# Linear attention of a decoder layer: the products of two heads in one group, alternating between two PSUM banks, in new slots

## The chip, the cores and the metric

One core of a Trainium2 chip runs the whole layer. The metric is device time in microseconds (us) of one execution. Three executions of the kernel before took 1095.80, 1095.86 and 1096.29 us; the median is 1095.86 us.

## What is computed

One layer on 512 tokens of width 1024: a feed-forward network, a mixer, a second feed-forward network, each between norms. The mixer has eight heads of softmax attention with forget gates ("fox") and four heads of gated linear attention ("gla"), in chunks of 64 tokens. The change is in the gla heads alone:

```python
q_in = qc * jnp.exp(b)
k_in = kc * jnp.exp(-b)
k_st = kc * jnp.exp(b_last - b)
attn = jnp.where(tril, jnp.einsum('bhncd,bhnsd->bhncs', q_in, k_in), 0.0)
o_intra = jnp.einsum('bhncs,bhnsv->bhncv', attn, vc)
kv = jnp.einsum('bhnsd,bhnsv->bhndv', k_st, vc)
...
o = o_intra + jnp.einsum('bhncd,bhndv->bhncv', q_in, s_prev)
```

The state `s_prev` is a scan over the eight chunks: decay times the state, plus that chunk's `kv`. The output of each head is then divided by its root mean square. A gla key head has 64 features, a value head 128.

## The kernel before

TensorE (PE), VectorE (DVE), ScalarE (ACT), GpSimd (POOL) and SyncE (SP) each run their own list of instructions, in the order of the code, and meet at semaphores (`wait_ge`). Weights come in units of 128x1024; ACT rounds each (`w_hi`, line 515) and DVE takes the rest (`w_lo`, line 901), and most products are made three times, hi by hi, hi by lo and lo by hi.

The middle of the mixer is a loop over 38 **slots** (`for sl in range(SLOTS_B)`), written once per engine. Slot `sl` belongs to step `sl` of the 32 steps of fox (a head and a block of 128 queries; step `sl` has `sl % 4 + 1` blocks of keys). In this order a slot holds:

- PE: the scores of step `sl` (lines 1625 to 1628), which wait for the exponential of step `sl - 2`; up to three blocks of a "filler", a projection that is due anyway (lines 1385 to 1387, three matmuls a block; slots with `sl % 4` of 0, 1, 2, 3 have 3, 3, 2, 0 blocks from slot 16 on); the gla group of that slot; the transposes of the probabilities of step `sl - 2` (line 1699); after every fourth step the product with the values ("PV", line 1709).
- ACT: the exponential (line 774), the reading of a finished filler (708 or 710 for keys and queries, 789 for the gate `gr`), the rounding of the transposed probabilities (802), a half sum of PV (808) in slots with `sl % 4 == 0`, `of_hi` (812) in slots 13, 21, 29 and 37, the gla group's work, the scaling of the probabilities (843), the rounding of a weight unit (515) after a finished filler.
- DVE: the maximum (1255), the reciprocal (1259), the rest of the keys (1200, 1204) or the gate (1268), the rest of the transposed probabilities (1273), a half sum (1279) and `of_lo` (1284), the states (1295, 1298), the gated product (1317) in slots 25, 29, 33, 37, the norm's gain (1322) and rest (1324), the rest of a weight unit (901) one slot after its filler ended.

So each engine works through the slots in order, and a piece of ACT's slot 18 cannot start before all earlier pieces of ACT's slots are done.

The gla groups have these kinds: `kst` transposes the keys for the state (line 1655), `attn` is the 64x64 product of queries and keys of every chunk (line 1661, copied out by ACT in line 830, two copies a head, and masked by POOL in line 1812), `kv` is keys by values of seven chunks (line 1671, read by DVE's seven state operations), `o` is the output, first four 128-row products inside the chunks (line 1680), then seven products of 64 rows with the states (line 1684), and `ms` the mean of the squares of a head (lines 1689, 1690; ACT squares the output in line 833 and rounds it in 837, DVE makes its rest in 1324; ACT copies the mean out in line 840). Fillers aside, all of these are plain fp32, and each matmul of such a product stands twice in the trace: `o` of one head has 8 records of line 1680 and 14 of line 1684.

Before the change a group is one head (`attn`, `o`, `ms`) or one half of the chunks (`kv`: even chunks lie in rows 0 to 63, odd ones in rows 64 to 127). Heads 0 and 2 have their features in rows 0 to 63, heads 1 and 3 in rows 64 to 127. The groups take two PSUM banks in turn, and each waits until the reader of the group before the last is done:

```python
gla_steps = [("kst", 0), ("kst", 1)]
for j in range(2):
    gla_steps += [("attn", 2 * j), ("attn", 2 * j + 1), ("kv", 2 * j), ("kv", 2 * j + 1),
                  ("o", 2 * j), ("ms", 2 * j), ("o", 2 * j + 1), ("ms", 2 * j + 1)]
gla_slots = {14: (0,), 16: (1,), 17: (2, 3), 18: (4, 5), 20: (6,), 22: (7, 8), 24: (9, 10), 25: (11, 12),
             26: (13,), 28: (14,), 30: (15, 16), 32: (17,)}
```

After the loop PE waits for the last of the means, gains and transposed probabilities and goes on with the gates (line 1385 on).

Of the kernel before, what the change touches and what calls it, by code (L numbers as in the profile page):

```python
# [23 lines left out]
P = 128  # L24
# [75 lines left out]
def macaron_layer(nc, h_store, x_t, g1cols, x, w1g, w1u, w1d, g1post, gmpre, w_in, b_forget, w_alpha, b_alpha,  # L100
                  gla_g, w_bf, w_bg, w_out, gmpost, g2pre, w2g, w2u, w2d, g2post, out):
    with ExitStack() as ctx:
# [187 lines left out]
        def gain(g):  # L290
# [3 lines left out]
        gla_slots = {14: (0,), 16: (1,), 17: (2, 3), 18: (4, 5), 20: (6,), 22: (7, 8), 24: (9, 10), 25: (11, 12),  # L294
                     26: (13,), 28: (14,), 30: (15, 16), 32: (17,)}
# [25 lines left out]
        def gbank(g):  # L321
            return bank[:, B_GLA[g % 2 if g >= 2 else 0], :]
# [176 lines left out]
        def _(act):  # L499
# [220 lines left out]

            act.wait_ge(const_in, 16 * len(consts_dma))
# [45 lines left out]
            for sl in range(SLOTS_B):  # L767
# [48 lines left out]
                for g in gla_slots.get(sl, ()):  # L816
                    kind, n = gla_steps[g]
                    if kind == "kst":
                        act.wait_ge(kst_ready, n + 1)
                        nc.scalar.activation(kst_tok[:, 2 * n:2 * n + 2, :].rearrange("p t f -> p (t f)"),  # L820
                                             gbank(g), ACT.Copy).then_inc(kst_copied, 1)
                    if kind == "attn":
                        act.wait_ge(attn_ready, n + 1)
                        act.wait_ge(intra_zeroed, 1)
                        if n >= 2:
                            act.wait_ge(o_ready, n - 1)
                        src = gbank(g).rearrange("p (t c) -> p t c", t=TT)
# [3 lines left out]
                    if kind == "o":  # L831
                        act.wait_ge(o_ready, n + 1)
                        nc.scalar.activation(msq[:, n, :], gbank(g), ACT.Square).then_inc(sq_ready, 1)
                        act.wait_ge(sq_ready, n + 1)
                        if n:
                            act.wait_ge(gms_ready, n)
                        nc.scalar.activation(sq_hi, msq[:, n, :], ACT.Copy).then_inc(sq_hi_out, 1)
                    if kind == "ms":
                        act.wait_ge(gms_ready, n + 1)
                        nc.scalar.activation(msq[:, n, :], gbank(g), ACT.Copy).then_inc(ms_out, 1)  # L840
# [54 lines left out]
        def _(dve):  # L895
# [310 lines left out]

            for s in range(INPUT):
# [43 lines left out]
            for sl in range(SLOTS_B):  # L1251
# [33 lines left out]
                for g in gla_slots.get(sl, ()):  # L1285
                    kind, n = gla_steps[g]
                    if kind == "kv" and n % 2:
                        j = n // 2
                        dve.wait_ge(kv_ready, n + 1)
                        if j:  # L1290
                            dve.wait_ge(o_ready, 2)
                        for c in range(NCH - 1):
                            kv = gbank(g - 1 + c % 2)[:, (c // 2) * GLA_DV:(c // 2 + 1) * GLA_DV]
                            if c == 0:
                                V.tensor_copy(state[:, 1, :], kv).then_inc(state_ready, 1)
                            else:
                                dve.wait_ge(state_ready, j * (NCH - 1) + c)
                                V.scalar_tensor_tensor(state[:, c + 1, :], state[:, c, :], decay[:, j, c:c + 1],
                                                       kv, ALU.mult, ALU.add).then_inc(state_ready, 1)
# [18 lines left out]
                for g in gla_slots.get(sl, ()):  # L1318
                    kind, n = gla_steps[g]
                    if kind == "o":  # L1320
                        dve.wait_ge(sq_ready, n + 1)
                        V.tensor_scalar(arena[:, T_OG[n], :], gbank(g), gn[:, n:n + 1], None, ALU.mult).then_inc(on_ready, 1)
                        dve.wait_ge(sq_hi_out, n + 1)
                        V.tensor_tensor(sq_lo, msq[:, n, :], sq_hi.bitcast(F32), ALU.subtract).then_inc(sq_lo_out, 1)
# [49 lines left out]
        def _(pe):  # L1374
# [211 lines left out]
            for s in range(4, INPUT):  # L1586
# [10 lines left out]
                for kk in range(2):  # L1597
# [14 lines left out]
            read = {"kst": lambda n: (kst_copied, n + 1), "attn": lambda n: (attn_copied, 2 * n + 2),  # L1612
                    "kv": lambda n: (state_ready, (NCH - 1) * (n // 2 + 1)), "o": lambda n: (on_ready, n + 1),
                    "ms": lambda n: (ms_out, n + 1)}
            for sl in range(SLOTS_B):
# [20 lines left out]
                for g in gla_slots.get(sl, ()):  # L1636
                    kind, n = gla_steps[g]
                    if g == 0:
                        pe.wait_ge(gv_out, TT)
                        pe.wait_ge(a_dve, 6)  # L1640
                    if g in (1, 2):
                        pe.wait_ge(kst_copied, g)
                    if g == 2:
                        pe.wait_ge(a_dve, 7)
                    if g == 3:
                        pe.wait_ge(k_lo, 2 * FOX_H // 2)
                    if g >= 4:
                        pk, pn = gla_steps[g - 2]
                        pe.wait_ge(*read[pk](pn))
                    dst = gbank(g)  # L1650
                    if kind == "kst":
                        for t in (2 * n, 2 * n + 1):
                            for j in range(2):
                                c = (t % 2) * 2 * P + j * P
                                last = nc.tensor.transpose(dst[:, c:c + P], arena[:, T_KST + j, t * P:(t + 1) * P], ident[:, :])
                        last.then_inc(kst_ready, 1)
                    if kind == "attn":
                        rows = slice(64 * (n % 2), 64 * (n % 2) + 64)
                        for t in range(TT):
                            toks = slice(t * P, (t + 1) * P)  # L1660
                            last = mm(dst[:, toks], arena[rows, T_GK + n // 2, toks], arena[rows, T_GQ + n // 2, toks],
                                      start=True, stop=True)
                        last.then_inc(attn_ready, 1)
                    if kind == "kv":
                        j, part_n = n // 2, n % 2
                        pe.wait_ge(kst_copied, 2)
                        for c in range(part_n, NCH - 1, 2):
# [191 lines left out]
```

## Time and profile before

| | |
|---|---|
| median of three runs | 1095.86 us |
| the profiled execution | 1095.99 us, its span 1094.2 us |
| PE (matmuls) busy | 1077.5 us, 98% |
| DVE, ACT, POOL busy | 667.9, 503.5, 34.6 us |
| all matmul and weight load instructions | 6558 each |
| PE's share of the chain that ended last | 87% |

The span runs from the first to the last instruction. PE's busy time is that of overlapping records: a matmul of 512 columns stands with 0.39 us and the next one starts 0.23 us after it. So the time that a group takes is read from the start of its first record to the start of the next group's first.

### The profile page before, as it was taken

To read this page: it belongs to the slowest core of one execution; us is meant where nothing else is said; L and a number is where in the kernel's file an instruction comes from. 1 tells how busy PE (TensorE), PEld (TensorE's weight loads), DVE (VectorE), ACT (ScalarE), POOL (GpSimd) and SP (SyncE) were. 2 spreads that over 40 slices of the span, in tenths; PEclk is the share of its full clock that TensorE was granted. 3 is DMA by queue.
4 is the path that set the end of the run, shared out by engine and by line. 5 is a ranking of instruction groups with operands and counts; after the bars stand their busy time and mean duration, and the time that the engine had idled before them with its cause. 6 is when DMAs were issued, how large, how long until landed. Compare 5 with 4: busy or idle time off the path is not lost.

```text
span 1094.2 us, 15984 instructions
## 1 busy us (share of the span) xinstructions
PE 1077.5 (98%) x6558; PEld 960.9 (88%) x6558; DVE 667.9 (61%) x809; ACT 503.5 (46%) x728; POOL 34.6 (3%) x76
## 2 busy tenths in 40 slices
PE   7999999999999999999999999999999999999997
PEld 5899999998888978888888888889899999988886
DVE  6788888873334663476655233458778787853334
ACT  7355455452223573667773222344454545442222
POOL 2000000000001100000000000011000000000001
PEclk9999999999999999999999999999999999999999
DMA  9622422434322544222114335315424234143311
GB/s 288 193 78 78 155 78 83 149 97 173 96 80 58 174 118 118 74 77 78 40 39 138 101 99 172 105 40 173 155 79 153 78 95 138 77 169 118 98 39 77
DMA packets 115203, 121.13 MB, mean 111 GB/s; under 512 B 6192, under 2 KB 100416, under 8 KB 115136
## 3 DMA queue, kind: packets, MB, share of 16 engines
q1 hardware_dynamic: 112960, 115.47, 34.0%
q10 hardware_dynamic: 1456, 2.10, 0.9%
q0 software_dynamic: 720, 2.62, 0.7%
q8 instruction: 47, 0.77, 0.3%
q14 instruction: 20, 0.16, 0.0%
HBM read 111.80 MB, written 6.29 MB: 108 GB/s over the span
## 4 chain that ended last, share of the span: by engine, by line
PE 87%; DVE 6%; ACT 2%; issue 2%; DMA 2%; POOL 1%; SPq 1%; ACTq 0%; DVEq 0%; POOLq 0%
PE bank L1395 25%; PE bank L1481 11%; PE bank L1483 11%; PE bank L1482 11%; PE bank L1385 6%; PE bank L1387 6%; PE bank L1386 6%; PE bank L1603 1%; PE bank L1604 1%; PE bank L1605 1%; DVE w_lo L901 1%; PE bank L1450 1%; PE bank L1451 1%; PE bank L1452 1%; DMA raw<-in_ffn_w_up 1%
## 5 line engine op out<-in xcount | busy, mean ns | idle before, releaser
L1481 PE MATMUL bank<-tc,w_hi 128*128 128x256 f32 x576 | 163.1, 283 | 0.3 <-ACT scr L606 0.3
L1482 PE MATMUL bank<-tc,w_hi 128*128 128x256 f32 x576 | 163.0, 283 | 0.0
L1483 PE MATMUL bank<-tc,w_lo 128*128 128x256 f32 x576 | 163.0, 283 | 0.0
L901 DVE TENSOR_TENSOR w_lo<-raw,w_hi 128x1024 fp32r<-128x1024 f32 x72 | 87.8, 1221 | 98.1 <-ACT w_hi L515 98.0
L1395 PE MATMUL bank<-w_hi,a_hi 128*128 128x512 f32 x408 | 126.1, 390 | 0.0
L1395 PE MATMUL bank<-w_hi,a_lo 128*128 128x512 f32 x408 | 125.6, 389 | 0.0
L1395 PE MATMUL bank<-w_lo,a_hi 128*128 128x512 f32 x408 | 125.6, 389 | 0.0
L1385 PE MATMUL bank<-u_hi,w_hi 128*128 128x512 f32 x312 | 123.6, 396 | 0.2 <-issue 0.2
L1481 PE MATMUL bank<-u_hi,w_hi 128*128 128x256 f32 x432 | 122.4, 283 | 1.3 <-DVE scr L1028 1.3
L1015 DVE TENSOR_TENSOR w_lo<-raw,w_hi 128x1024 fp32r<-128x1024 f32 x36 | 44.1, 1226 | 129.3 <-ACT w_hi L593 129.3
L1483 PE MATMUL bank<-u_hi,w_lo 128*128 128x256 f32 x432 | 122.3, 283 | 0.0
L1482 PE MATMUL bank<-u_lo,w_hi 128*128 128x256 f32 x432 | 122.2, 283 | 0.0
L1387 PE MATMUL bank<-u_hi,w_lo 128*128 128x512 f32 x312 | 121.8, 390 | 0.0
L1386 PE MATMUL bank<-u_lo,w_hi 128*128 128x512 f32 x312 | 121.6, 390 | 0.0
L1481 PEld LDWEIGHTS bank<-tc,w_hi 128*128 128x128 f32 x576 | 110.6, 192 | 0.5 <-ACT scr L606 0.5
L1482 PEld LDWEIGHTS bank<-tc,w_hi 128*128 128x128 f32 x576 | 110.6, 192 | 0.0
L1483 PEld LDWEIGHTS bank<-tc,w_lo 128*128 128x128 f32 x576 | 110.6, 192 | 0.0
L515 ACT ACTIVATE w_hi<-raw 128x1024 fp32r<-128x1024 f32 x72 | 75.8, 1054 | 57.1 <-PE bank L1387 24.3
L593 ACT ACTIVATE w_hi<-raw 128x1024 fp32r<-128x1024 f32 x36 | 38.2, 1060 | 138.1 <-PE bank L1395 138.1
L1009 DVE TENSOR_TENSOR w_lo<-raw,w_hi 128x1024 fp32r<-128x1024 f32 x60 | 73.2, 1222 | 29.8 <-ACT w_hi L587 29.8
L1395 PEld LDWEIGHTS bank<-w_lo,a_hi 128*128 128x128 f32 x408 | 76.6, 188 | 16.0
L1395 PEld LDWEIGHTS bank<-w_hi,a_lo 128*128 128x128 f32 x408 | 76.6, 188 | 15.9
(235 smaller groups left out, 2068.7 us busy)
## 6 DMA issues: line engine op xcount, KB each, us to landing
raw<-in_w_in SPq DMA_DIRECT2D x40, 512.0 KB, 3.8
raw<-in_ffn_w_down SPq DMA_DIRECT2D x36, 512.0 KB, 3.5
raw<-in_ffn_w_gate SPq DMA_DIRECT2D x10, 1024.0 KB, 5.4
raw<-in_ffn_w_up SPq DMA_DIRECT2D x10, 1024.0 KB, 8.0
h<-in_ffn_w_gate SPq DMA_DIRECT2D x8, 1024.0 KB, 5.4
h<-in_ffn_w_up SPq DMA_DIRECT2D x8, 1024.0 KB, 8.3
raw<-in_ffn_w_up SPq DMA_DIRECT2D x8, 512.0 KB, 5.2
h<-in_x SPq DMA_DIRECT2D x8, 512.0 KB, 6.9
```

The lines of the kernel that those rows point to most:

```text
L515: nc.scalar.activation(w_hi[:, slot(u), :], raw[:, slot(u), :], ACT.Copy).then_inc(hi_ready, 1)
L593: nc.scalar.activation(w_hi[:, slot(u), :], raw_down(layer, n), ACT.Copy).then_inc(hi_ready, 1)
L901: V.tensor_tensor(w_lo[:, slot(u), :], raw[:, slot(u), :], w_hi[:, slot(u), :].bitcast(F32), ALU.subtract).then_inc(lo_ready, 1)
L1009: V.tensor_tensor(w_slot(w_lo, u), w_source(q, n), w_slot(w_hi, u).bitcast(F32), ALU.subtract).then_inc(lo_ready, 1)
L1015: V.tensor_tensor(w_lo[:, slot(u), :], raw_down(layer, n), w_hi[:, slot(u), :].bitcast(F32), ALU.subtract).then_inc(lo_ready, 1)
L1385: mm(dst, w_hi[:, slot(u), w], rhs_hi[:, k - k0, :], start=k == k0, stop=False)
L1386: mm(dst, w_hi[:, slot(u), w], rhs_lo[:, k - k0, :], start=False, stop=False)
L1387: last = mm(dst, w_lo[:, slot(u), w], rhs_hi[:, k - k0, :], start=False, stop=k == k1)
L1395: last = mm(bank[:, 2 * t + c, :], a[:, s, toks], w[:, s, c * HALF:(c + 1) * HALF], start=first and a is a_hi and w is w_hi, stop=final an ...
L1481: mm(dst, w_hi[:, slot(u), w], moving(n, 0, k), start=first and k == 0, stop=False, skip_group_check=True)
L1482: mm(dst, w_hi[:, slot(u), w], moving(n, 1, k), start=False, stop=False, skip_group_check=True)
L1483: last = mm(dst, w_lo[:, slot(u), w], moving(n, 0, k), start=False, stop=k == KD // 2 - 1, skip_group_check=True)
```

## The change

The two heads of a pair now make one group, and their instructions alternate: `attn` and the state products of `o` go by token tile or chunk, head 0 of the pair (rows 0 to 63, bank 1) and head 1 (rows 64 to 127, bank 2) in turn. `kv` takes the seven chunks in order, so that rows 0 to 63 and rows 64 to 127 alternate. `ms` stays one head a group. The table of slots has one group a slot. The operations and their number are the same. On ACT and DVE the rounding and the rest of the squares of the second head of a pair move from the `o` group to the `ms` group of the first head.

```diff
-        gla_steps = [("kst", 0), ("kst", 1)]
-        for j in range(2):
-            gla_steps += [("attn", 2 * j), ("attn", 2 * j + 1), ("kv", 2 * j), ("kv", 2 * j + 1),
-                          ("o", 2 * j), ("ms", 2 * j), ("o", 2 * j + 1), ("ms", 2 * j + 1)]
...
-        gla_slots = {14: (0,), 16: (1,), 17: (2, 3), 18: (4, 5), 20: (6,), 22: (7, 8), 24: (9, 10), 25: (11, 12),
-                     26: (13,), 28: (14,), 30: (15, 16), 32: (17,)}
+        gla_slots = {14: ("kst", 0), 16: ("kst", 1), 18: ("attn", 0), 19: ("kv", 0), 21: ("o", 0), 23: ("ms", 0), 24: ("ms", 1),
+                     26: ("attn", 1), 27: ("kv", 1), 29: ("o", 1), 31: ("ms", 2), 32: ("ms", 3)}
...
-        def gbank(g):
-            return bank[:, B_GLA[g % 2 if g >= 2 else 0], :]
+        def gbank(e):
+            return bank[:, B_GLA[e], :]
...
+                    for e in range(2):
+                        src = gbank(e).rearrange("p (t c) -> p t c", t=TT)
                         for c in range(2):
                             rows = slice(c * CHUNK, (c + 1) * CHUNK)
-                            nc.scalar.activation(intra[rows, n % 2, :, rows], src[rows, :, rows], ACT.Copy).then_inc(attn_copied, 1)
...
+                            nc.scalar.activation(intra[rows, e, :, rows], src[rows, :, rows], ACT.Copy).then_inc(attn_copied, 1)
+                if kind == "o":
+                    act.wait_ge(o_ready, n + 1)
+                    for e in range(2):
+                        nc.scalar.activation(msq[:, 2 * n + e, :], gbank(e), ACT.Square).then_inc(sq_ready, 1)
+                    squares_rounded(2 * n)
+                if kind == "ms":
+                    act.wait_ge(gms_ready, n + 1)
+                    if n % 2 == 0:
+                        squares_rounded(n + 1)
+                    nc.scalar.activation(msq[:, n, :], gbank(n % 2), ACT.Copy).then_inc(ms_out, 1)
...
+                if kind == "o":
+                    for e in range(2):
+                        h_n = 2 * n + e
+                        dve.wait_ge(sq_ready, h_n + 1)
+                        V.tensor_scalar(arena[:, T_OG[h_n], :], gbank(e), gn[:, h_n:h_n + 1], None, ALU.mult).then_inc(on_ready, 1)
+                    squares_rest(2 * n)
+                if kind == "ms" and n % 2 == 0:
+                    squares_rest(n + 1)
...
+                    for t in range(TT):
+                        toks = slice(t * P, (t + 1) * P)
+                        for e in range(2):
+                            rows = slice(64 * e, 64 * e + 64)
+                            last = mm(gbank(e)[:, toks], arena[rows, T_GK + n, toks], arena[rows, T_GQ + n, toks],
                                       start=True, stop=True)
...
+                if kind == "kv":
+                    pe.wait_ge(attn_copied, 4 * n + 4)
+                    for c in range(NCH - 1):
+                        rows = slice(CHUNK * (c % 2), CHUNK * (c % 2) + CHUNK)
...
+                if kind == "o":
+                    pe.wait_ge(attn_masked, 4 * n + 4)
+                    pe.wait_ge(state_ready, (NCH - 1) * (n + 1))
...
+                    for c in range(1, NCH):
+                        cols = slice(c * CHUNK, (c + 1) * CHUNK)
+                        for e in range(2):
+                            rows = slice(64 * e, 64 * e + 64)
+                            last = mm(gbank(e)[:, cols], state[rows, c, :], arena[rows, T_GQ + n, cols],
                                       start=False, stop=c == NCH - 1, skip_group_check=True)
...
+                if kind == "ms":
+                    pe.wait_ge(on_ready, n + 1)
+                    pe.wait_ge(sq_lo_out, n + 1)
```

`squares_rounded` and `squares_rest` are ACT's and DVE's operations on the squares, line for line as before, in functions of their own.

What stands in a row now, in three places. First ACT from slot 17 to slot 18 (names: `scr` holds probabilities and small tiles, `pt` the transposed probabilities, `qk` the heads of keys and queries). Before:

```order
L774 ACTIVATE scr,rowsum<-bank,neg_max 128x256 [waits pt_ready,max_ready]
L802 ACTIVATE pt<-bank 128x4x128 [waits pv_done,pt_ready]
L830 ACTIVATE scr<-bank 64x4x64 [waits intra_zeroed,attn_ready]
L830 ACTIVATE scr<-bank 64x4x64
L830 ACTIVATE scr<-bank 64x4x64 [waits intra_zeroed,attn_ready]
L830 ACTIVATE scr<-bank 64x4x64
L843 ACTIVATE scr<-scr,rinv 128x256 [waits rinv_ready]
L774 ACTIVATE scr,rowsum<-bank,neg_max 128x384 [waits pt_ready,max_ready]
L710 ACTIVATE qk<-bank 64x512 [waits scores_ready,unit_used]
L710 ACTIVATE qk<-bank 64x512
L802 ACTIVATE pt<-bank 128x128 [waits pv_done,pt_ready]
L843 ACTIVATE scr<-scr,rinv 128x384 [waits rinv_ready]
```

With the change:

```order
L776 ACTIVATE scr,rowsum<-bank,neg_max 128x256 [waits pt_ready,max_ready]
L804 ACTIVATE pt<-bank 128x4x128 [waits pv_done,pt_ready]
L845 ACTIVATE scr<-scr,rinv 128x256 [waits rinv_ready]
L776 ACTIVATE scr,rowsum<-bank,neg_max 128x384 [waits pt_ready,max_ready]
L705 ACTIVATE qk<-bank 64x512 [waits scores_ready,unit_used]
L705 ACTIVATE qk<-bank 64x512
L804 ACTIVATE pt<-bank 128x128 [waits pv_done,pt_ready]
L832 ACTIVATE scr<-bank 64x4x64 [waits intra_zeroed,attn_ready]
L832 ACTIVATE scr<-bank 64x4x64 x3
L845 ACTIVATE scr<-scr,rinv 128x384 [waits rinv_ready]
```

The four copies (line 830, now 832) stood in slot 17, ahead of the next exponential; now they stand in slot 18, behind its exponential, the two operations on the queries and the rounding.

Second, PE at the same place, from the `attn` group to the transposes behind `kv`, with the change:

```order
L1662 MATMUL bank<-arena 128x128 [waits k_lo,a_dve,kst_copied]
L1662 MATMUL bank<-arena 128x128 x7
L1703 MATMUL bank<-ident,scr 128x128 [waits pt_lo,probs_ready]
L1628 MATMUL bank<-qk 128x512 [waits exp_done]
L1629 MATMUL bank<-qk 128x512
L1630 MATMUL bank<-c_neg,head_sel 128x512
L1631 MATMUL bank<-causal,ident_r 128x128
L1671 MATMUL bank<-arena,scr 64x128 [waits attn_copied]
L1671 MATMUL bank<-arena,scr 64x128 x13
L1703 MATMUL bank<-ident,scr 128x128 [waits pt_lo,probs_ready]
```

Before, a scores group and two filler blocks stood between `attn` and `kv`, and `kv` waited for two of the four copies at its head and for all four half way. Now only one transpose and the scores stand between them, and the first `kv` matmul waits for all four copies.

Third, PE from the `o` group in slot 21 to the first `ms` in slot 23, with the change:

```order
L1687 MATMUL bank<-arena,scr 128x64 x14
L1703 MATMUL bank<-ident,scr 128x128 [waits pt_lo,probs_ready]
L1703 MATMUL bank<-ident,scr 128x128 x3
...
L1703 MATMUL bank<-ident,scr 128x128 [waits pt_lo,probs_ready]
L1628 MATMUL bank<-qk 128x512 [waits exp_done]
L1629 MATMUL bank<-qk 128x512
L1630 MATMUL bank<-c_neg,head_sel 128x512
L1631 MATMUL bank<-causal,ident_r 128x128
L1693 MATMUL bank<-a_hi,mean_g 128x512 [waits sq_lo_out,on_ready]
```

The lines left out are slot 22's scores and two filler blocks. Before, `o` of head 0 stood in slot 20 and its `ms` in slot 22, with five filler blocks between them.

## Rows read from the trace of the kernel before

**Rows 1.** Windows: start:end, length, then busy us and count by engine, clock, DMA.

```profile
495.95:557.38 61.43, 61.05 (x416) 52.38 (x414) 40.08 (x89) 43.67 (x101) 3.76 (x8) 1.00 0.16 44
```

**Rows 2.** Timeline of PE, slots 17 to 23: start, us, engine, line, operation, tiles.

```profile
499.10 1.71 PE L1661 MATMUL bank<-arena 64*128 64x128 f32 x16 [0.38 <-ACT scr L820]
500.74 0.66 PE L1699 MATMUL bank<-ident,scr 128*128 128x128 f32 x4
...
504.73 0.48 PE L1625 MATMUL bank<-qk 128*128 128x512 f32 x1
...
505.57 0.39 PE L1699 MATMUL bank<-ident,scr 128*128 128x128 f32 x2
505.72 1.47 PE L1709 MATMUL bank<-pt,og 128*128 128x512 f32 x8
...
515.63 0.42 PE L1625 MATMUL bank<-qk 128*128 128x384 f32 x1
...
517.73 0.39 PE L1689 MATMUL bank<-a_hi,mean_g 128*128 128x512 f32 x1
...
520.88 0.33 PE L1699 MATMUL bank<-ident,scr 128*128 128x128 f32 x1
```

**Rows 3.** Chain that ended last, slots 18 to 26: start, us, what.

```profile
503.42 1.30 PE bank L1671 x28
...
509.78 0.97 PE bank L1680 x8
510.75 1.70 PE bank L1684 x14
...
526.44 1.08 PE bank L1661 x8
...
531.61 1.02 PE bank L1671 x16
...
535.24 0.80 PE bank L1671 x12
```

**Rows 4.** Timeline of ACT, slots 17, 18 and 22 to 23.

```profile
500.64 0.48 ACT L774 ACTIVATE scr<-bank,neg_max 128x256 f32<-128x256 f32 x1 [1.31 <-DVE neg_max L1255]
...
501.43 0.60 ACT L802 ACTIVATE pt<-bank 128x512 fp32r<-128x512 f32 x1 [0.23 <-PE bank L1699]
501.92 1.58 ACT L830 ACTIVATE scr<-bank 64x256 f32<-64x256 f32 x4
...
504.06 0.58 ACT L774 ACTIVATE scr<-bank,neg_max 128x384 f32<-128x384 f32 x1
...
504.63 1.20 ACT L710 ACTIVATE qk<-bank 64x512 fp32r<-64x512 f32 x2
505.85 0.28 ACT L802 ACTIVATE pt<-bank 128x128 fp32r<-128x128 f32 x1
...
523.57 1.04 ACT L515 ACTIVATE w_hi<-raw 128x1024 fp32r<-128x1024 f32 x1
524.85 0.69 ACT L774 ACTIVATE scr<-bank,neg_max 128x512 f32<-128x512 f32 x1 [0.23 <-DVE neg_max L1255]
```

**Rows 5.** Timeline of DVE, slots 17, 22, 23 to 25.

```profile
502.06 0.69 DVE L1273 TENSOR_TENSOR pt<-bank,pt 128x512 fp32r<-128x512 f32 x1 [0.66 <-ACT pt L802]
502.67 0.55 DVE L1255 TENSOR_REDUCE neg_max<-bank 128x1 f32<-128x384 f32 x1
...
523.53 0.68 DVE L1324 TENSOR_TENSOR a_lo<-scr,a_hi 128x512 fp32r<-128x512 f32 x1
...
526.28 1.22 DVE L901 TENSOR_TENSOR w_lo<-raw,w_hi 128x1024 fp32r<-128x1024 f32 x1
...
529.83 0.41 DVE L1255 TENSOR_REDUCE neg_max<-bank 128x1 f32<-128x256 f32 x1
```

**Rows 6.** Timeline of PE at the start of the program.

```profile
7.63 1.22 PE L1553 MATMUL bank<-u_hi,w_hi 128*128 128x512 f32 x2 [7.63 <-ACT u_hi L683]
...
12.89 0.62 PE L1553 MATMUL bank<-u_hi,w_hi 128*128 128x512 f32 x2
```

More of the change, by code:

```diff
@@ L719, in spread_keys, with squares_rounded @@
                                   qk[rows, p % 2, KH[e]:KL[e] + 1, :].bitcast(F32)).then_inc(k_spread[p], 16)
+            def squares_rounded(n):
+                act.wait_ge(sq_ready, n + 1)
+                if n:
+                    act.wait_ge(gms_ready, n)
+                nc.scalar.activation(sq_hi, msq[:, n, :], ACT.Copy).then_inc(sq_hi_out, 1)
             act.wait_ge(const_in, 16 * len(consts_dma))
@@ L815, in _ @@
                     nc.scalar.activation(ga, gb, ACT.Exp, scale=-1.0 / TAU).then_inc(a_act, 1)
[L816 to L827, printed above, removed]
+                kind, n = gla_slots.get(sl, (None, 0))
@@ new lines, in _ @@
+                if kind == "kst":
+                    act.wait_ge(kst_ready, n + 1)
+                    nc.scalar.activation(kst_tok[:, 2 * n:2 * n + 2, :].rearrange("p t f -> p (t f)"),
+                                         gbank(0), ACT.Copy).then_inc(kst_copied, 1)
+                if kind == "attn":
+                    act.wait_ge(attn_ready, n + 1)
+                    act.wait_ge(intra_zeroed, 1)
+                    if n:
+                        act.wait_ge(o_ready, n)
+                    for e in range(2):
+                        src = gbank(e).rearrange("p (t c) -> p t c", t=TT)
@@ L1635, in _ @@
                         last.then_inc(unit_used, 1)
-                for g in gla_slots.get(sl, ()):
-                    kind, n = gla_steps[g]
-                    if g == 0:
+                kind, n = gla_slots.get(sl, (None, 0))
+                if kind == "kst":
+                    if n:
+                        pe.wait_ge(kst_copied, 1)
+                    else:
                         pe.wait_ge(gv_out, TT)
                         pe.wait_ge(a_dve, 6)
-                    if g in (1, 2):
-                        pe.wait_ge(kst_copied, g)
-                    if g == 2:
+                    for t in (2 * n, 2 * n + 1):
+                        for j in range(2):
+                            c = (t % 2) * 2 * P + j * P
+                            last = nc.tensor.transpose(gbank(0)[:, c:c + P], arena[:, T_KST + j, t * P:(t + 1) * P], ident[:, :])
+                    last.then_inc(kst_ready, 1)
@@ L1644, in _ @@
+                if kind == "attn":
+                    if n:
+                        pe.wait_ge(ms_out, 2)
+                    else:
+                        pe.wait_ge(kst_copied, 2)
                         pe.wait_ge(a_dve, 7)
-                    if g == 3:
                         pe.wait_ge(k_lo, 2 * FOX_H // 2)
[L1647 to L1661, printed above, removed]
-                                      start=True, stop=True)
[L1663 to L1667, printed above, removed]
-                            rows = slice(CHUNK * part_n, CHUNK * part_n + CHUNK)
-                            for e in range(2):
-                                hh = 2 * j + e
-                                last = mm(dst[64 * e:64 * e + 64, (c // 2) * P:(c // 2 + 1) * P],
-                                          kst_tok[rows, c // 2, hh * GLA_DK:(hh + 1) * GLA_DK],
-                                          arena[rows, T_GV + c // 2, hh * GLA_DV:(hh + 1) * GLA_DV], start=True, stop=True)
-                        last.then_inc(kv_ready, 1)
@@ new lines, in _ @@
+                    last.then_inc(attn_ready, 1)
+                if kind == "kv":
+                    pe.wait_ge(attn_copied, 4 * n + 4)
+                    for c in range(NCH - 1):
+                        rows = slice(CHUNK * (c % 2), CHUNK * (c % 2) + CHUNK)
+                        for e in range(2):
+                            hh = 2 * n + e
+                            last = mm(gbank(c % 2)[64 * e:64 * e + 64, (c // 2) * P:(c // 2 + 1) * P],
+                                      kst_tok[rows, c // 2, hh * GLA_DK:(hh + 1) * GLA_DK],
+                                      arena[rows, T_GV + c // 2, hh * GLA_DV:(hh + 1) * GLA_DV], start=True, stop=True)
+                    last.then_inc(kv_ready, 1)
```

73 lines of the change are left out of this document (23 added, 50 removed).

## The prediction

> **What bounds the kernel now.** I read the windows first, then PE's timeline slot by slot, then the chain of waits, then ACT and DVE at the same places. In slots 17 to 32, where all changed groups but the key transposes lie, PE is busy 61.05 of 61.43 us at the full clock, ACT 43.67, DVE 40.08 [rows 1]. The one wait of PE there is 0.38 us, for ACT's copy of the transposed keys [rows 2]. So PE sets the pace, and what its groups save is saved, as long as the other two stay ahead. They have a third of the time free, but they work in slot order too, and a result that PE needs comes only after all that stands before it.
>
> **What PE saves.** A piece of the chain lasts until the next piece starts, so its times add up.
>
> - `attn`: one head alone is 1.08 us (8 records), two heads one behind the other in slot 17 are 1.71 [rows 2, 3]. So the second head, in the other 64 rows, already runs partly beside the first. Fully alternating, a pair takes what one head takes, 1.1. Pair 0 saves 0.6, pair 1 (two groups in two slots) 1.1.
> - `kv`: 28 records together took 1.30, apart 1.02 and 0.80 [rows 3]. The even chunks (16 records) are the longer half, and the odd ones lie in other rows and another bank, so a pair takes 1.02: it saves 0.3 and 0.8.
> - `o`: 0.97 for the four 128-row products of a head, 1.70 for its 14 records with the states [rows 3]. The first stay (128 rows have no second half). Of the second, no row shows two heads at once. If nothing overlaps, the saving is 0; nothing excludes a small loss. If all does, it is 1.70 a pair. The nearest row is `attn`, the same 64 rows by 128 columns of weights in two row halves and two banks, and 16 records in 1.71 where 8 take 1.08 can't be had without overlap. I take 3.4 for both pairs.
> - Three fewer groups of 64-row products and two fewer `o` groups are entered, at about 0.1 each by the first product of a group: 0.3, with overlaps counted once. The 0.38 wait goes with its cause, since the copy of slot 16 is long done when slot 18 asks: 0.4.
>
> Sum: 0.6 + 1.1 + 0.3 + 0.8 + 3.4 + 0.3 + 0.4 = **6.9 us** saved.
>
> **What it waits for instead.** No operation of ACT or DVE is removed; they move.
>
> Slot 19, `kv` of pair 0, needs all four copies of `attn`. PE arrives early: slot 17's transposes follow its fillers at 498.6 (499.10 less the wait and 0.1 of entering), slot 18 takes 0.4 for those, 2.1 for scores and two blocks (515.63 to 517.73), 1.2 for the pair and 0.1 for a transpose, slot 19's scores 0.84 (504.73 to 505.57) [rows 2]: 503.2. ACT: the exponential of slot 17 stays at 500.64, since the maximum that it waits for hangs on older work. The rounding follows at 501.2 instead of 501.43, DVE starts its rest 0.63 later as before (501.43 to 502.06) at 501.8, and the maximum of slot 18 0.6 after that (502.06 to 502.67) at 502.4 [rows 4, 5]. Then exponential at 503.0, queries at 503.6 (504.06 to 504.63), rounding at 504.8 (504.63 to 505.85), copies from 505.0, 1.6 long [rows 4]: done at 506.6. Before, they began at 501.92. **PE waits 3.3 us**, and behind its first `kv` matmul stand two transposes, PV and all of slot 20.
>
> Slot 23, first `ms`, needs the rest of the squares. Before, after `o` of head 1, this rest ended at 524.2, that is 3.3 after PE's next transpose at 520.88 [rows 2, 5]. Now DVE first has one more gain operation and `of_lo`, each about 0.6 (one such 128x512 operation is 0.68 with its overlap [rows 5]), so 4.5 and 0.1 to pass the signal. PE meanwhile has transposes 0.4, slot 22 with 2.1 and 0.1, and scores 0.84: 3.5. **Wait 1.1.**
>
> Slot 24, second `ms`, needs the rest of head 1's squares, now made in slot 23. ACT and DVE hand on in turn, each start from the one before: maximum 0.6, exponential 0.6, gate 0.5, rounding 0.2, scaling 0.5, weight unit 1.0, exponential 0.7 [rows 4], rounding 0.3, squares 0.6, rest 0.7: 5.7. PE from the first `ms` on: 0.5 for it, 0.2 transposes, 1.3 PV (1.47 less its overlap) [rows 2], 0.4 scores, 2.1 three blocks: 4.5. **Wait 1.1** once a signal's 0.1 is taken off both.
>
> Slot 27, `kv` of pair 1: the chain from that rest runs over a weight unit to the maximum of slot 25 in 3.55 (526.28 to 529.83, a piece in which before, too, PE was not waited for) [rows 5], then 2.8 over exponential, rounding, its rest and the gated product to the maximum of slot 26, then 3.4 to the end of the copies as in slot 18, with the gate's 0.5 for the queries' 1.2: 9.8. PE: 0.7 for `ms` and transposes, 3.0 slot 25, 3.4 slot 26, 0.9 scores: 8.0. **Wait 1.7.** Slot 31 is slot 23 again with one gated product, 0.6, in front of the gain: **1.7**. Slot 32 is slot 24 again, with no scores on PE (0.4 less to hide behind), and its filler may wait for the gate's DVE operation inside the same sum: **1.5**.
>
> Hidden: the four kst transposes, POOL's masks (they run while PE still waits), and the states, since DVE has about 7 us for its 2.5 before `o` in slot 21. After the loop, the chain over ACT (two table loads, logarithm, exponential) and DVE starts from the last PV and moves with it, so the gates keep their distance. DMA queues are untouched; loads are released by weight units that come a few us later, and each lands in about 4.
>
> Waits: 3.3 + 1.1 + 1.1 + 1.7 + 1.7 + 1.5 = **10.4**, less 6.9 saved: **+3.5 us**. The profiled execution took 1095.99, the median is 0.13 lower. Forecast 1095.86 + 3.5 = **1099.4 us**. The waits hang on sums of ten small steps; with 0.3 us of error in each, and each wait shifting the next, the forecast's own range is 1097 to 1102.
>
> The Trainium skill (TensorEngine Tiling, PSUM Bottleneck) says that tiling the array speeds up TensorE but not the emptying of PSUM, which may become the bottleneck. Were the emptying free, the sum would be the first rival's.
>
> **Rivals.**
>
> 1. PE stays the bound. For it: only 0.38 us of wait in 61 [rows 1, 2]. Then the time is 1095.9 - 6.9 = 1089.0. It decides by the copies of slot 18: they would have to end by 503.2, but ACT has 2.0 us of exponential, queries and rounding ahead of them there [rows 4]. Chance 0.07.
> 2. Faster, by one mechanism: only slot 19's wait is real, and after it ACT and DVE, which had 3.3 us to drain their lists, stay ahead to the end. 1095.9 - 6.9 + 3.3 = 1092.3. It decides by the rest of the squares: if it ends within 3.5 us of `o`, there is no wait. Against it: the transposes of slot 21 stand behind `o` on PE, and ACT can't square before it has rounded them, so a lead doesn't help. Chance 0.13. Between this and the forecast, with each later wait at half, lies 1095.9; chance 0.08.
> 3. The clock. At the start, after 7.6 us without a matmul, two matmuls take 1.22 us, and from 12.89 on 0.62 [rows 6]: the lower level, 1.2 GHz, for about 4.5 us. If 3.3 us of idling in slot 19 brings it back, what follows takes up to 2.3 longer: 1101.7. The longest wait in rows 1 is 0.38, so no row says. Chance 0.12. The Trainium skill (TensorE: Matmul & The Clock Gate, Why this matters for your kernels) warns that a gap between bursts of matmuls puts the engine back to that level.
> 4. The change doesn't do what it says: the halves don't run side by side in `o`. Then 3.4 of the saving are gone: 1102.8. Chance 0.04.
>
> **How the numbers follow.** About 0.2%, 2.2 us, is what can be told from no change here. The forecast has 0.56. Of it some 0.07 lies within 2.2 us of before. Slower: 0.49 + 0.12 + 0.04, 0.65. Same: 0.07 + 0.08, 0.15. Faster: 0.07 + 0.13, 0.20. The range leaves out rival 1 and a part of rivals 3 and 4, and takes in rival 2: 1092.0 to 1102.8. Both signs have weight, and the likeliest case alone is 1097 to 1102.
>
> **What would show it.** PE, `kv`: 3.3 us idle before its first record in slot 19, released by ACT's copies; 1.7 in slot 27. Waits of 1 to 2 us before each `ms`, released by DVE's rest. Pairs of line 1687's records a few ns apart, 14 pairs in 1.7 us; the `attn` pair in 1.1. No idle time before `o` beyond 0.1. The clock in all windows 1.00. It is wrong if ACT's copies in slot 18 start before 504, if the rest of the squares ends within 3.5 us of the end of `o`, or if line 1687's 28 records take over 2 us.

## The result, and the profile after

| | before | after |
|---|---|---|
| median of 5 runs each, side by side | 1095.81 us | 1101.03 us |
| lowest to highest | 1095.64 to 1096.29 | 1100.5 to 1102.56 |
| profiled execution, its span | 1095.99 us, 1094.2 us | 1101.03 us, 1099.3 us |
| ratio after to before, 95% interval | | 1.0047 [1.0036, 1.0058] |

The change makes the kernel slower, by 5.2 us, where 3.5 had been forecast; 1101.03 lies inside the range. Now and then an execution is slow as a whole (1512 to 5499 us here, mostly at a lower clock), and the medians below leave such executions out. The page of the changed kernel, its head, its line for each engine, and the shares of the chain that ended last:

```profile
span 1099.3 us, 15976 instructions
...
PE 1073.3 (98%) x6558; PEld 956.5 (87%) x6558; DVE 668.1 (61%) x809; ACT 502.3 (46%) x728; POOL 34.2 (3%) x76
...
PE 84%; DVE 7%; ACT 3%; issue 2%; DMA 2%; POOL 1%; SPq 1%; ACTq 0%; DVEq 0%; POOLq 0%
```

Before, PE was busy 1077.5 us and held 87% of the chain. It now works less and the kernel takes longer. The windows of after: slots 17 to 32 as in [rows 1], then three short stretches around slot 19 (the columns are those of [rows 1]: after the length come PE, PEld, DVE, ACT and POOL, then the clock):

```profile
496.10:562.47 66.37, 57.06 (x416) 48.00 (x414) 41.05 (x89) 42.69 (x101) 3.30 (x8) 0.97 0.15 41
...
502.35:506.36 4.01, 1.08 (x7) 0.73 (x5) 2.90 (x7) 3.17 (x9) 0.42 (x2) 1.00 0.38 110
506.36:509.76 3.40, 3.10 (x32) 2.67 (x33) 0.44 (x3) 3.06 (x7) 1.24 (x3) 0.50 0.01 2
509.76:513.20 3.44, 3.44 (x21) 2.95 (x21) 3.23 (x9) 0.52 (x1) 0.00 (x0) 1.00 0.00 0
```

The same 416 records of PE are busy 57.06 us instead of 61.05, but the stretch is 66.37 long instead of 61.43: 9.3 us of it is idle, where there was 0.4. And for 3.40 us from 506.36 on the clock is at its lower level, 1.2 GHz. What PE waits for around these slots, in total us, times, longest:

```profile
PE bank L1671 <- ACT scr L832: 4.6, 2, 3.2
PE bank L1693 <- DVE a_lo L1212: 4.5, 4, 1.7
PE bank L1391 <- DVE arena L1275: 0.2, 1, 0.2
```

L1671 is `kv`, released by the copies of `attn`; L1693 is `ms`, released by the rest of the squares. PE's timeline shows where each stands; compare it with [rows 2] and [rows 3]:

```profile
501.25 1.16 PE L1662 MATMUL bank<-arena 64*128 64x128 f32 x16
502.35 0.33 PE L1703 MATMUL bank<-ident,scr 128*128 128x128 f32 x1
...
503.21 0.22 PE L1631 MATMUL bank<-causal,ident_r 128*128 128x128 f32 x1
506.66 1.97 PE L1671 MATMUL bank<-arena,scr 64*64 64x128 f32 x28 [3.23 <-ACT scr L832]
508.56 0.69 PE L1703 MATMUL bank<-ident,scr 128*128 128x128 f32 x2
508.90 1.87 PE L1713 MATMUL bank<-pt,og 128*128 128x512 f32 x8
...
517.94 1.78 PE L1687 MATMUL bank<-arena,scr 64*128 64x64 f32 x28
519.65 0.66 PE L1703 MATMUL bank<-ident,scr 128*128 128x128 f32 x4
...
524.33 0.48 PE L1693 MATMUL bank<-a_hi,mean_g 128*128 128x512 f32 x1 [1.14 <-DVE a_lo L1212]
...
529.84 0.47 PE L1693 MATMUL bank<-a_hi,mean_g 128*128 128x512 f32 x1 [0.77 <-DVE a_lo L1212]
...
539.33 1.09 PE L1671 MATMUL bank<-arena,scr 64*64 64x128 f32 x28 [1.38 <-ACT scr L832]
540.35 0.44 PE L1703 MATMUL bank<-ident,scr 128*128 128x128 f32 x2
...
556.15 0.47 PE L1693 MATMUL bank<-a_hi,mean_g 128*128 128x512 f32 x1 [1.74 <-DVE a_lo L1212]
558.54 0.47 PE L1391 MATMUL bank<-u_hi,w_hi 128*128 128x512 f32 x1 [0.23 <-DVE arena L1275]
561.67 0.47 PE L1693 MATMUL bank<-a_hi,mean_g 128*128 128x512 f32 x1 [0.81 <-DVE a_lo L1212]
```

All three products of a pair run abreast: `attn` of a pair in 1.10 us from start to next start (501.25 to 502.35), `kv` in 1.02 where the clock is full (539.33 to 540.35), the state products of both heads in 1.71 (517.94 to 519.65), as long as one head took before [rows 3]. In slot 19, at half the clock, the same 28 records of `kv` take 1.97 instead of 1.09, both with their overlap, and PV 1.87 instead of 1.47 [rows 2].

ACT's timeline says why slot 19 waits (to be read against [rows 4]):

```profile
500.79 0.47 ACT L776 ACTIVATE scr<-bank,neg_max 128x256 f32<-128x256 f32 x1 [1.30 <-DVE neg_max L1262]
...
503.07 0.58 ACT L776 ACTIVATE scr<-bank,neg_max 128x384 f32<-128x384 f32 x1 [0.83 <-DVE neg_max L1262]
503.64 1.19 ACT L705 ACTIVATE qk<-bank 64x512 fp32r<-64x512 f32 x2
504.86 0.28 ACT L804 ACTIVATE pt<-bank 128x128 fp32r<-128x128 f32 x1
505.03 1.57 ACT L832 ACTIVATE scr<-bank 64x256 f32<-64x256 f32 x4
```

The products are there at 502.35. ACT is even idle 0.83 us before 503.07, but its next instruction in order is an exponential that waits for DVE, and the copies stand behind that, the queries and a rounding: 505.03 to 506.60.

### The profile page after: what moved, and what is told of

Read it like the earlier page. It is cut to its first block, busy times and chain, and to the rows that moved or that the text cites. A ratio compares the mean times of both kernels' runs of the same rounds, so it can differ in the third digit from the quotient of the medians.

```text
span 1099.3 us, 15976 instructions
## 1 busy us (share of the span) xinstructions
PE 1073.3 (98%) x6558; PEld 956.5 (87%) x6558; DVE 668.1 (61%) x809; ACT 502.3 (46%) x728; POOL 34.2 (3%) x76
## 4 chain that ended last, share of the span: by engine, by line
PE 84%; DVE 7%; ACT 3%; issue 2%; DMA 2%; POOL 1%; SPq 1%; ACTq 0%; DVEq 0%; POOLq 0%
PE bank L1401 25%; PE bank L1487 11%; PE bank L1489 10%; PE bank L1488 10%; PE bank L1391 6%; PE bank L1393 6%; PE bank L1392 6%; PE bank L1609 1%; PE bank L1610 1%; PE bank L1611 1%; DVE w_lo L903 1%; PE bank L1456 1%; PE bank L1458 1%; PE bank L1457 1%; DMA raw<-in_ffn_w_up 1%
```

## The experiments

Two theories to begin with. **Theory A**: the pairs save what was said, and the moved steps cost it back in waits, to which half a clock in slot 19 adds 1.5 us. **Theory B**, as it stands in the first expectations: the alternating products themselves are what costs time, and the slots matter little. A weaker form of it is tested too: the pairs are worth little, since two heads one behind the other overlapped already. All experiments are edits of the changed kernel but e9. Each figure is a median, with the ratio to the kernel before, run beside it (1095.78 for e1 to e4, 1095.68 for e5 to e8, 1095.84 for e9), and its 95% interval.

### e1: `attn` and `kv` of pair 0 a slot earlier

```diff
-14: ("kst", 0), 16: ("kst", 1), 18: ("attn", 0), 19: ("kv", 0), 21: ("o", 0), ...
+14: ("kst", 0), 16: ("kst", 1), 17: ("attn", 0), 18: ("kv", 0), 21: ("o", 0), ...
```

> Only the first pair's attn and kv go back to slots 17 and 18; all else is the changed kernel. Theory A (the loss is waits of TensorE for results that the other engines make in slot order): ScalarE's four copies stand in slot 17 again and end near 503.4, so the 3.2 us wait before kv shrinks to 0.2 to 0.6, the clock stays at its full level (1.4 us more), and the 0.4 us wait for the key copy returns: 1101.0 - 3.0 - 1.4 + 0.4, about 1097.0 us, with the waits before the means (4.5 us together) and before the second kv (1.4) as they are. Theory B (the alternating products themselves are what costs time): the slots matter little, 1101 us to within 1.

Measured: **1098.02 us**, 1.0019 [1.0009, 1.0029]: 3.0 less than after. PE's timeline of e1, `kv` of pair 0, the scores of slot 21, `kv` of pair 1:

```profile
503.17 1.09 PE L1671 MATMUL bank<-arena,scr 64*64 64x128 f32 x28 [0.34 <-ACT scr L832]
...
510.55 0.39 PE L1628 MATMUL bank<-qk 128*128 128x256 f32 x1 [0.92 <-ACT scr L776]
...
536.47 1.09 PE L1671 MATMUL bank<-arena,scr 64*64 64x128 f32 x28 [1.33 <-ACT scr L832]
```

The wait of 3.23 is down to 0.34 and the clock stays full, which is worth 2.9 and 1.5. Given back are 0.9 before the scores of slot 21, a wait that was hidden behind the large one, and 0.4 for the transposed keys, the wait of [rows 2]. 2.9 + 1.5 - 0.9 - 0.4 = 3.1. The strong form of theory B, 1101 to within 1, falls.

### e4: the wait filled with work

Before `kv` of pair 0, behind the scores of slot 19 in its list, PE does twelve products into PV's bank, once that has been read (`pair_ready`). PV then overwrites them. Nothing else is changed.

```diff
                 if kind == "kv":
+                    if n == 0:
+                        pe.wait_ge(pair_ready, 3)
+                        for _ in range(12):
+                            mm(bank[:, B_OT, :], ident_r[:, :], u_hi[:, 0, :], start=True, stop=True)
                     pe.wait_ge(attn_copied, 4 * n + 4)
```

> The changed kernel with twelve 128x512 matmuls (2.8 us) into the bank of PV, which PV overwrites afterwards, in front of kv's wait in slot 19; their result is not used. They fill TensorE's idle time of 3.2 us and hold up nothing. If the half clock that follows that idle time is caused by it, the granted clock stays at 1.00 throughout, kv takes 1.1 us instead of 2.0, and the time falls by 1.3 to 1.6 us, to about 1099.6. If the lower clock has another cause, it stays in the trace and the time is 1101.0 or more.

Measured: **1099.54 us**, 1.0037 [1.0023, 1.0051]: 1.5 less than after, with twelve products more to do. PE's timeline and the windows of e4:

```profile
502.91 3.01 PE L1669 MATMUL bank<-u_hi,ident_r 128*128 128x512 f32 x12
...
506.28 1.09 PE L1675 MATMUL bank<-arena,scr 64*64 64x128 f32 x28 [0.36 <-ACT scr L832]
...
507.50 1.47 PE L1717 MATMUL bank<-pt,og 128*128 128x512 f32 x8
```

```profile
502.20:507.00 4.80, 4.44 (x43) 3.43 (x44) 2.89 (x6) 4.17 (x11) 1.31 (x4) 1.00 0.28 79
507.00:510.20 3.20, 3.20 (x30) 2.80 (x23) 1.37 (x5) 2.55 (x5) 0.34 (x1) 1.00 0.00 0
```

`kv` starts when the copies are done, as in after, but at the full clock, and it and PV take 1.09 and 1.47 again. From `kv`'s first record to the scores of slot 20 PE takes 2.53 us (506.28 to 508.81), in after 3.95 (506.66 to 510.61). So the wait had two prices: 3.2 us of itself, and 1.4 to 1.5 behind it.

### e2: the pairs in the slots from before

```diff
-..., 18: ("attn", 0), 19: ("kv", 0), 21: ("o", 0), 23: ("ms", 0), 24: ("ms", 1),
-26: ("attn", 1), 27: ("kv", 1), 29: ("o", 1), 31: ("ms", 2), 32: ("ms", 3)}
+..., 17: ("attn", 0), 18: ("kv", 0), 20: ("o", 0), 22: ("ms", 0), 24: ("ms", 1),
+25: ("attn", 1), 26: ("kv", 1), 28: ("o", 1), 30: ("ms", 2), 32: ("ms", 3)}
```

Each step stands in a slot where a group of its kind stood before (`attn` and `kv` of pair 1 in the later of two); only the pairs are new.

> The alternating pairs of the changed kernel in the slots where the kernel before had the first of its groups: attn 17 and 25, kv 18 and 26, o 20 and 28, means 22, 24, 30, 32. Theory A: nearly all waits go; left are 0.4 us for the key copy, up to 0.4 us before each kv and 0.2 before o, and the saving of 6.7 us of TensorE shows: 1089 to 1091 us. Theory B: not below 1095.8 us, the time of the kernel before.

Measured: **1094.86 us**, 0.9992 [0.9982, 1.0002]. A miss: 1089 to 1091 had been expected, and this can't be told from before. The waits of after are gone, but others have come:

```profile
PE bank L1391 <- DVE arena L1275: 2.5, 2, 1.8
PE bank L1662 <- ACT scr L842: 1.0, 1, 1.0
PE bank L1662 <- ACT scr L821: 0.4, 1, 0.4
PE bank L1671 <- ACT scr L832: 0.3, 1, 0.3
```

PE starts PV of slot 31 at 549.77, where before it started at 553.23: 3.5 earlier. That is the 5.9 us which the pairs save by busy and idle time (see below), less 2.4 of waits. The windows of e2 over what follows, and PE's timeline there:

```profile
549.70:553.05 3.35, 1.54 (x10) 1.34 (x11) 2.29 (x7) 2.02 (x6) 0.00 (x0) 1.00 0.00 0
553.79:557.20 3.41, 3.41 (x9) 2.52 (x8) 2.10 (x4) 2.64 (x6) 0.00 (x0) 0.50 0.00 0
```

```profile
549.77 1.47 PE L1713 MATMUL bank<-pt,og 128*128 128x512 f32 x8
...
553.05 0.47 PE L1391 MATMUL bank<-u_hi,w_hi 128*128 128x512 f32 x1 [1.81 <-DVE arena L1275]
```

The filler behind it is the last gate's, and all fillers share one bank. It waits 1.8 us until DVE's gate operation has read the one before it, which itself waits for ACT; and the clock falls again, for 3.41 us, at a price of half of that, 1.7. The gates at the end start at 563.34, before at 563.22. The executions seem to fall apart by this: four with a mean clock of 0.998 have a median of 1095.8, five with 0.999 or 1.0 one of 1094.3. Only one of the four has a trace, so for the others the same fall is inferred from their mean.

### e3 and e6: the heads one behind the other

The edit, in the slots of e2 (e3) and in those of after (e6); `o` is turned in the same way, and `kv` takes the even chunks first:

```diff
-                    for t in range(TT):
-                        for e in range(2):
+                    for e in range(2):
+                        for t in range(TT):
...
-                    for c in range(NCH - 1):
+                    for c in (0, 2, 4, 6, 1, 3, 5):
```

> As e2, but in each group one head (in kv: the even chunks) is issued wholly before the other, so that only the alternation is undone. If alternation is what lets the row halves run abreast, the groups take attn 2.1, kv 1.8, state products 3.4 us, and the time is 6.0 us over e2. If TensorE looks ahead in its queue, as the 1.71 us of attn in slot 17 of the kernel before suggests, the second head starts about 0.6 us after the first and the loss is 0.6 us a group of attn and of state products and 0.3 a kv: 3 us over e2, near 1093.

> The changed kernel in its own slots, with the alternation alone undone. In e3 a group without alternation took 0.55 (attn), 0.28 (kv) and 1.16 us (state products) longer. attn is hidden here, since kv waits for copies that wait for other work of ScalarE; kv and the state products are not: 2 x (0.28 + 1.16) = 2.9, so 1104 us. If the changed kernel's loss came from the alternation, this would be faster than 1101.0.

Measured: e3 **1098.13 us**, 1.0026 [1.0014, 1.0038], 3.3 over e2; e6 **1104.17 us**, 1.0076 [1.0058, 1.0094], 3.1 over after. PE's timeline of e3, `attn`, `kv` and the state products:

```profile
499.17 1.71 PE L1662 MATMUL bank<-arena 64*128 64x128 f32 x16 [0.38 <-ACT scr L821]
...
503.62 1.37 PE L1671 MATMUL bank<-arena,scr 64*64 64x128 f32 x28
...
511.76 2.94 PE L1687 MATMUL bank<-arena,scr 64*128 64x64 f32 x28
```

Against 1.16, 1.09 and 1.78: 0.55, 0.28 and 1.16 a pair, 4.0 for both pairs. The traced execution of e3 keeps the full clock; it took 1098.27, which is 4.0 over the 1094.3 of e2's executions at the full clock. So in the old slots nearly all of it reaches the end. In e6 the wait before `kv` in slot 19 hides `attn`'s part. The weaker theory B falls too: the alternation is worth 3 to 4 us wherever the steps stand. But it has a part of the truth, since the state products of two heads took 2.94 one behind the other in one slot, and not 2 x 1.70. The rest of what PE saves comes from both heads being in one slot at all.

These two traces also bear on the clock. PE's timeline of e6 at `kv` of pair 0, then a window behind it; and PE's timeline of e3 at the last gate's filler:

```profile
506.82 1.82 PE L1671 MATMUL bank<-arena,scr 64*64 64x128 f32 x28 [2.66 <-ACT scr L832]
```

```profile
507.59:511.00 3.41, 3.41 (x27) 2.88 (x20) 1.38 (x5) 2.53 (x5) 0.29 (x1) 0.50 0.00 0
```

```profile
556.81 0.47 PE L1391 MATMUL bank<-u_hi,w_hi 128*128 128x512 f32 x1 [1.82 <-DVE arena L1275]
```

In e6 the clock falls behind 2.66 us of idling. In e3 it stays at 1.00 behind 1.82, in the very place where it fell in e2 behind 1.81.

### e5: only the means and `o` late

```diff
-17: ("attn", 0), 18: ("kv", 0), 21: ("o", 0), 23: ("ms", 0), 24: ("ms", 1), 26: ("attn", 1), 27: ("kv", 1), ...
+17: ("attn", 0), 18: ("kv", 0), 21: ("o", 0), 23: ("ms", 0), 24: ("ms", 1), 25: ("attn", 1), 26: ("kv", 1), ...
```

The lines with a minus are e1's. This is e1 with pair 1's `attn` and `kv` a slot earlier too.

> As e2, but o and the means stay in the changed kernel's slots (o 21 and 29, means 23, 24, 31, 32). Theory A: kv's waits stay as in e2 (0.3), and the four waits before the means come back with 4 to 4.5 us. They use up nearly all that e2 saved, so slot 33 starts 1 to 2 us later than in the kernel before: 1096.5 to 1098. If the waits before the means are not a matter of those slots, the trace shows them under 1 us in total and the time is that of e2, 1095.2.

Measured: **1097.22 us**, 1.0014 [1.0004, 1.0024]. What PE waits for in e5:

```profile
PE bank L1693 <- DVE a_lo L1212: 4.5, 4, 1.7
PE bank L1628 <- ACT scr L776: 0.9, 1, 0.9
PE bank L1671 <- ACT scr L832: 0.3, 1, 0.3
```

The 1.3 us of slot 27 are gone, and 0.8 of them at the end. The waits of the means are the same 4.5 us in after, e1, e5 and e6, whatever comes before them, and none of them is in e2. The distance in slots is not what counts: in e2 the first `ms` also follows `o` by two slots (20 and 22, 28 and 30), but with five filler blocks between them, where slots 21 to 23 and 29 to 31 have two. The second `ms` follows the first by two slots in e2 and by one here. Each time the squares' chain over ACT and DVE has to be gone through, and it is hidden only if PE has that much work ahead of `ms`.

### e7: e2, with the last filler in a bank of its own

```diff
         def fill_bank(f):
+            if f == len(FILLERS) - 1:
+                return B_S[0]
...
+            if f == len(FILLERS) - 1:
+                return (exp_done, NS - 1)
```

It goes to a bank of the scores, free once the last exponential has read it, and waits for no gate operation.

> As e2, but the last filler (the projection of the fourth gate, slots 32 to 34) writes the bank of the even scores, free once step 30's exponential is done, instead of the bank that VectorE must first read for the third gate. In e2 TensorE waits 1.8 us for that, and in part of the runs the clock then falls. Theory: this wait is what pins the end of the loop to the place it had before the change. Then it shrinks to about 0.7 (the exponential ends 1.2 us before the gate's operation), the clock stays full, and the time falls by 1.2 us against e2's undisturbed runs (1094.2) to 1093.0. If ScalarE's and VectorE's lists alone pin the end, nothing changes: 1094.2 to 1095.2.

Measured: **1093.48 us**, 0.9979 [0.9969, 0.9989], 1.4 under e2 and faster than before. PE's timeline of e7, the first record of that filler:

```profile
551.45 0.47 PE L1395 MATMUL bank<-u_hi,w_hi 128*128 128x512 f32 x1 [0.61 <-ACT scr L780]
```

The wait is 0.6 us instead of 1.8, so the filler starts 1.2 us earlier, counted from PV's start (2.07 behind it instead of 3.28), and the clock of this trace stays full. Against e2's executions at the full clock (1094.3) the gain is 0.8: a new wait of 0.46 before PV of slot 35, for DVE's rest of the probabilities, takes a part back. So the one bank held e2 back by 0.8 us, and by 1.5 more where the clock fell.

### e9: the same bank in the kernel before

The edit of e7, made in the kernel before.

> The kernel before with the one other edit of e7: the last filler writes the bank of the even scores. In the kernel before TensorE had no wait there, so the bank alone is worth nothing: within 0.3 us of 1095.7. If it falls by 1 us or more, e7's gain over e2 is not the wait that the pairs expose, but something that the kernel before could have had without them.

Measured: **1095.75 us** against 1095.84, 0.9997 [0.9988, 1.0007]. So the bank alone is worth nothing where PE comes to the filler late; it becomes a bound only behind the pairs.

### e8: three more moves in e7

The second transposed keys move to slot 15, the gated product of head 1 from slot 29 to 31, and ACT's copy of the second mean goes ahead of slot 24's exponential. Each is aimed at one wait of e7.

```diff
-14: ("kst", 0), 16: ("kst", 1), 17: ("attn", 0), ...
+14: ("kst", 0), 15: ("kst", 1), 17: ("attn", 0), ...
-        gated_slots = {25: 0, 29: 1, 33: 2, 37: 3}
+        gated_slots = {25: 0, 31: 1, 33: 2, 37: 3}
...
+                if gla_slots.get(sl) == ("ms", 1):
+                    act.wait_ge(gms_ready, 2)
+                    nc.scalar.activation(msq[:, 1, :], gbank(1), ACT.Copy).then_inc(ms_out, 1)
```

> As e7, with three more moves: the second key transpose in slot 15 instead of 16 (0.4 us of wait before attn in slot 17), ScalarE's copy of the second mean ahead of slot 24's exponential (1.0 us of wait before attn in slot 25), the gated product of head 1 in slot 31 instead of 29 (0.6 us earlier maximum of slot 30). Each is worth its wait if TensorE stays the bound to the end: 1091 us. If the end is pinned by the other engines, it is e7's time.

Measured: **1092.80 us**, 0.9971 [0.996, 0.9983], the fastest of all: 2.9 under the kernel before and 8.2 under the changed one, but not the 1091 that had been expected. What PE waits for in e8:

```profile
PE bank L1678 <- ACT scr L839: 1.6, 2, 1.3
PE bank L1720 <- DVE pt L1287: 0.8, 1, 0.8
PE bank L1398 <- DVE arena L1282: 0.6, 1, 0.6
```

The key copy's 0.4, `attn`'s 1.0 and the last filler's 0.6 are gone, but `kv` in slot 18 now waits 1.3 where it waited 0.3. PE is there earlier, and the copies are later. ACT's timeline of e8 shows why:

```profile
495.13 0.59 ACT L828 ACTIVATE scr<-bank 128x512 f32<-128x512 f32 x1
```

This is the copy of the transposed keys. It stands in slot 15 now, ahead of the rounding of a weight unit and of slot 16's exponential, and both start 0.5 us later than in e7 (counted from slot 14's key transposes, as all of what follows). So do the copies of `attn`, and so does PE's slot 19: the first move took out 0.4 and cost 1.0. Behind it the waits of 1.0 and 0.6 are gone and the one before PV of slot 35 grows from 0.5 to 0.8; 0.7 us in all reach the end. It shows again that ACT's list sets the time of slot 18.

## Why the prediction was right, and where it was off

- **The saving** was said to be 6.9. The products came out as taken: `attn` 1.10 (1.1), `kv` 1.02 (1.02), 28 state records in 1.71 (1.70, the end of the range that full overlap gives; rival 4 falls). PE is busy 57.06 instead of 61.05, and 1.5 of that is time at half the clock, so 5.5, and the 0.4 of the key copy is gone as well: 5.9.
- **The waits** were said to be 10.4. Measured as idle time, with the forecast behind each: slot 19 3.23 (3.3), slot 23 1.14 (1.1), slot 24 0.77 (1.1), slot 27 1.38 (1.7), slot 31 1.74 (1.7), slot 32 0.23 + 0.81 (1.5). The sum is 9.3. Six waits in six places, each with the releaser named. ACT's copies were put from 505.0 to 506.6 and ran from 505.03 to 506.60.
- Both sums seem about 1 us too large, and the net is not: without the clock it is (66.37 - 61.43) - 1.5 = 3.4, for a forecast of 3.5. The difference is one of counting. The forecast counts from start to start. Idle time counts from the end of the last record, and that end lies 0.16 us behind the place where the next record would have started: in slot 19 the last record ends at 503.43, and the next would have started at 503.27, by the 0.06 us after which the record behind line 1628's starts in the trace of before (553.02 and 553.08). With 0.16 for each of the seven idle times, which is an estimate from this one place, the waits are 10.4 and the saving 7.0. The agreement of the sums is closer than that of their parts: the single waits are then off by up to 0.2 us, in both directions, and that this cancels is luck.
- **The step that failed is rival 3**, the clock, held at 0.12 and priced at up to 2.3. It was no rival to the forecast but a term of it: the clock was at the lower level for 3.40 us from 506.36, and took 1.5 us, by e4. In a sum it reads 3.5 + 1.5 = 5.0, and 5.2 was measured. By the trace alone it is 1.4, and up to 2.3 had been the price, since PE was at the lower level for 3.10 us of work and not for 4.5. The prediction had the row for it, the slow matmuls after the idle start [rows 6], and no row between 0.4 and 7.6 us of idling to place 3.3; the forecast's "clock in all windows 1.00" was a choice without a row. The rule of the Trainium skill that the prediction set beside it (TensorE: Matmul & The Clock Gate, Why this matters for your kernels) was borne out by this trace, with 3.23 us idle and 0.50 granted behind it.
- **The first rival** (PE stays bound) falls by the wait in slot 19. But the time that it priced, 1089.0, is not reached by e2 or e8 either, which have no wait over 1.9: there the gate's filler, ACT's list and `attn`'s bank become bounds of 0.3 to 1.8 us each. None of the orders tried got the saving of 6.9 as a whole; e8 gets 2.9.
- **The second rival** (only slot 19's wait is real, 1092.3) falls by the four waits of the means, 4.5 us in every kernel that has them there. The argument given against it, that a lead doesn't help since the chain starts from `o`, is what e1, e5 and e6 show.

What stays open is when the clock falls. It fell behind 3.23 us of idling in after, at 506.35, while PE still waited; behind 2.66 in e6, 0.8 us after PE had gone on; and behind 1.81 in the traced execution of e2, 0.7 us after. It did not fall behind 1.74 in after (slot 31) and behind 1.82 in e3, in the same place as in e2. So the length of the gap alone doesn't decide, and what does is not shown.

## What to carry to other kernels

A pair of products that share an array is worth what it saves on PE only if the engines that feed the next step are moved with it: when PE gets shorter in a kernel whose ACT and DVE run fixed lists, write down for each moved step when the last operation ahead of its own in those lists ends, and you have the waits, here to within 0.5 us each. An operation moved forward in such a list delays all that stands behind it (e8's first move). Separate the two halves of a change, the faster products (here 3 to 4 us by alternation alone) and the new places of the steps, and keep the old places first. A wait of PE of some us may be charged twice, once as itself and once in the clock behind it, so it is the first to take out; and a resource with one buffer, such as the fillers' bank, costs nothing until the work ahead of it gets short (nothing in e9 against before, 0.8 us or more in e7 against e2).

## What the runs showed of the hardware that was not expected

**TensorE overlaps two row halves that are not written side by side.** In e3 the four `attn` products of the first head stand wholly ahead of those of the second. A head's records start every 0.11 us in the trace, once its first is under way. 0.55 us after the first record, while three of the first head's eight are still to start, a second series with the same spacing begins, and 16 records take 1.71 us where 8 take 1.08. In the trace of before the same is seen in slot 17, and there one record can be told apart: the last of the first head, which raises the semaphore for that head, starts at 499.98, and the second head's series began at 499.65. The 28 state records take 2.94 in this order and 1.71 to 1.78 alternating. So the alternation is worth less than the count of products says, 1.2 us for 28 records instead of 1.7. The Trainium skill (TensorE: Matmul & The Clock Gate, What overlaps and what doesn't) has weight loads overlap running matmuls in other row groups, which agrees with this, but has matmuls start strictly in program order, which these starts do not show (499.65 ahead of 499.98); the measurement decides.

**Filling a wait with useless products paid.** Twelve products that nobody reads, 3.01 us of PE, made the kernel 1.5 us faster (1101.03 to 1099.54). The trace shows that the 28 + 2 + 8 records behind them kept the full clock.
